# Two products of each pair swapped, and the last group's sums shared out between VectorE and GpSimd

## Chip, cores and metric

The kernel runs on one core of one Trainium2 chip. The metric is the device time of one execution in microseconds (us): 1793.84 us is the median of 3 runs of the kernel before (1793.82 to 1794.68).

In what follows PE is TensorE's matmul, DVE is VectorE, ACT is ScalarE, POOL is GpSimd, and SP is SyncE, which here only issues transfers.

## The reference

The layer count is one, so only the pooling mixer is used. All inputs are float32; the tokens are 2048 of one request and 512 of another, 1024 channels each, and the MLP is 4096 wide.

```python
def trunk(x, ...):
    h = rms_norm(x, norm_mix_g[0])
    y = pool_mixer(h, pool_w[0], pool_scale[0])   # centred means over 2, 4, 8, 16 tokens, less the token,
    x = x + y                                     # then a 256x256 product for each of 4 channel groups
    h = rms_norm(x, norm_mlp_g[0])
    a = relu(h @ w_up)                            # 1024 -> 4096
    x = x + (a * a) @ w_down                      # 4096 -> 1024
    return rms_norm(x, final_norm_g)
```

## The kernel before, in words

**Tiling.** The 2560 tokens are 5 groups of 512 (`GROUPS`; `LAST` is the fifth). The MLP's 4096 inner channels are taken 512 at a time: 8 steps per group (`PAIRS`), 40 steps in all (`STEPS`). A step n computes four up tiles (`up_tile(4n)` to `up_tile(4n+3)`, 24 matmuls each) and, beside them, the down product of step n-1. The last step's products stand alone at the end.

**Precision.** Every float32 operand is split in a high part (cast by ACT) and a low part (the difference, by DVE), and each product is three matmuls: high by high, high by low, low by high. `split_wu`, `split_w`, `split_a`, `split_h2` and `split_pooled` are such pairs, one half in ACT's program and one half of the same name in DVE's.

**Seven products.** The down product of a step is a 2x2 block product by Strassen's scheme in Winograd's form, with seven products P1 to P7 of 12 matmuls each in place of eight. Their order on PE is the tuple at line 39, `P1, P5, P6, P3, P4, P7, P2`. Left operands are quadrants of the activation `a_raw` or sums of them in one shared tile `s_sum`, which `sum_a` rewrites for P5, P6, P3 and P7 one after the other, each time when the product before has been split. Right operands are quadrants of `w_down` or sums of them (`sum_w`, tiles `t_sum` and `wd_raw`); those of the first group's 56 products are split once, stored to a cache in HBM by `store_w` and loaded again by `load_w` in later groups. SP issues both in the order of product numbers.

**Ring.** Products go to PSUM in pairs of banks, two pairs in turn (`ring_pair`). A product may start when the one two turns before it has been added by DVE to its accumulator in `m_acc` (`evict`); `ring_full` and `ring_read` count the two. `TURN` numbers the turns; in the steps that mix the next group's tokens two turns of the pooling product follow the sixth product.

**Combining.** After a group's eighth step, seven sums of 128x1024 (`combine(g, 1)` to `combine(g, 7)`, lines 844 to 866) turn the seven accumulators into four quadrants: P2 + P1 is the upper left; P3 + P5 + (P6 + P1) the upper right; with P7 + (P6 + P1) the lower left is that less P4, and the lower right is that plus P5. `evict` of the last step waits for those sums that must stand before it, since it adds to the same tile. Then, for each of four row tiles, ACT takes the mean square (`final_stats`, line 592), POOL takes the power -1/2 (`rms`, two small instructions), DVE multiplies by it and by the gain (`finish`), and SP stores. For groups 0 to 3 this lies in `boundary`, beside the next group's first step; for the last group it is the end of the kernel.

**Order.** Each engine has its own program, written out by hand: `step`, `boundary` and the lines after the loops. An engine executes in that order, and a waiting instruction holds everything behind it. In `boundary`, PE transposes the next group's normed tokens in four pairs of blocks (`transpose`), each pair ahead of one of the first four products; ACT and DVE split each block (`split_h2`, tiles h_hi and h_lo), and the first up tile waits for all eight. In the steps that mix, POOL takes the window sums (`window_sums`, line 346).

Of the kernel before, what the change touches and what calls it, by code (L numbers as in the profile page):

```python
# [6 lines left out]
P = 128  # L7
# [31 lines left out]
P1, P5, P6, P3, P4, P7, P2 = range(7)  # L39
# [23 lines left out]
FIRST_OUTS = WINDOWS * TT  # L63

# [16 lines left out]
def ring_turns():  # L81

    turns, at = {}, 0
    for n in range(STEPS + 1):
        for k in range(NP if n > 0 else 0):
            turns[NP * (n - 1) + k] = at
            at += 1
            if k == P7 and n < STEPS and pooled_window(n) is not None:
# [27 lines left out]
def build(nc, x, halos, w_up, w_down, pool_w, pool_scale, g_mix, g_mlp, g_fin, ends, bands, ident_in,  # L116
# [8 lines left out]
    with ctx:  # L125
# [66 lines left out]
        ms_f = sb("ms_f", [P, TT])  # L192
        me_f = sb("me_f", [P, TT])
# [90 lines left out]
        combined = sem("combined")  # L284
        p4_begun = sem("p4_begun")
# [70 lines left out]
        def _(sp):  # L356
# [50 lines left out]
            def store(g):  # L407
                for i, j in enumerate(end_order(g)):
# [71 lines left out]
        def _(act):  # L480
# [111 lines left out]
            def final_stats(g, r):  # L592

                squares = dt_hi[:, :, :]
                if r == 0:
                    act.wait_ge(combined, NP * g + 4)
                    act.wait_ge(ring_read, TURN[NP * (PAIRS * (g + 1) - 1) + P2] + 1)
                else:
                    act.wait_ge(combined, NP * (g + 1))
                for j in (2 * r, 2 * r + 1):  # L600
                    i = end_order(g).index(j)
                    if i > 0:
                        act.wait_ge(ms_f_done, TT * g + i)
                    nc.scalar.activation(squares, out_rows(j), ACT.Square, scale=D ** -0.5,
                                         accum_out=ms_f[:, j:j + 1]).then_inc(ms_f_done, 1)
# [100 lines left out]
            def boundary(n):  # L706
# [37 lines left out]
            for k in range(2, NP):  # L744
                split_a(NP * (STEPS - 1) + k)
            final_stats(LAST, 0)
            final_stats(LAST, 1)

        @block.vector
        def _(dve):  # L750
# [67 lines left out]
            def evict(q):  # L818
# [6 lines left out]
                if s == PAIRS - 1 and k in (P7, P2):  # L825
                    dve.wait_ge(combined, NP * g + {P2: 1, P7: 5}[k])
# [3 lines left out]
                if s > 0:  # L830
# [11 lines left out]
            def combine(g, i):  # L842
# [12 lines left out]
                elif i == 4:  # L855
                    dve.wait_ge(combined, NP * g + 3)
# [7 lines left out]
                elif i == 7:  # L864
                    dve.wait_ge(combined, NP * g + 6)
# [34 lines left out]
            def finish(g):  # L900
                dve.wait_ge(g_fin_in, 16)
                for i, j in enumerate(end_order(g)):
# [62 lines left out]
            def step(n):  # L965
# [5 lines left out]
                if n > 0:  # L971
# [42 lines left out]
            def boundary(n):  # L1014
# [16 lines left out]
                split_a(q0 + P3)  # L1031
                evict(q0 + P6)
                split_w(q0 + P4)
# [4 lines left out]
                split_w(q0 + P7)  # L1038
                evict(q0 + P3)
                split_a(q0 + P7)  # L1040
# [30 lines left out]
            combine(LAST, 1)  # L1071
# [340 lines left out]
```

## Time and profile before

| | |
|---|---|
| median of 3 runs | 1793.84 us |
| profiled execution, own time | 1795.25 us |
| profiled execution, span from first to last instruction | 1793.4 us |
| mean granted TensorE clock | 0.993 |
| PE busy | 1756.7 us (98% of the span) |
| DVE busy | 1123.0 us (63%) |
| ACT busy | 761.6 us (42%) |
| POOL busy | 158.9 us (9%) |

Busy time is the time in which at least one instruction of the engine ran; a busy PE is not PE at its peak. The times in the rows below are microseconds from the start of the span of the profiled execution. A row of a timeline has start, duration, engine, line of the source, operation, tile written <- tiles read, shape and count; in square brackets, where it is given, is the time that the engine stood idle before it and the instruction that ended the wait.

### The profile page before, as it was taken

Reading aid. Unit: us, or ns where it says so; the run is one execution under the profiler, and the core shown is the slowest. Engines: PE = TensorE matmul, PEld = TensorE weight load, DVE = VectorE, ACT = ScalarE, POOL = GpSimd, SP = SyncE. Lnnn points to the kernel's source line nnn. Section 1 sums busy time; section 2 is a strip of 40 time slices with the busy share of each in tenths; the row PEclk is TensorE's granted clock in tenths of the full one; section 3 lists DMA queues with packets and bytes.
Section 4 is the critical chain, followed back from the end, with each engine's and each line's share of the span. In section 5 each row is a group of like instructions: output and inputs, shape, how many; then the busy total and the mean of one; then the engine's idle time right before and its main releaser. Section 6 shows DMA issues by size and latency. Waiting matters only on the chain.

```text
span 1793.4 us, 20892 instructions
## 1 busy us (share of the span) xinstructions
PE 1756.7 (98%) x8118; PEld 1462.1 (82%) x8118; DVE 1123.0 (63%) x1178; ACT 761.6 (42%) x1186; POOL 158.9 (9%) x139
## 2 busy tenths in 40 slices
PE   8999999999999999999999999999999999999996
PEld 7887887778888888888888888888888888888885
DVE  5687888787555565755655647555556575545447
ACT  5546555554343334344433344443333543333232
POOL 3000112001001120010011200000112010000001
PEclk9999999999999999999999999999999999999998
DMA  7597766668866666668666665786665657666654
GB/s 256 209 343 272 265 256 251 256 241 324 298 236 221 221 223 219 244 231 297 239 221 221 222 219 200 274 301 221 222 222 210 240 201 273 245 219 240 233 201 163
DMA packets 80902, 432.67 MB, mean 241 GB/s; under 512 B 8860, under 2 KB 10780, under 8 KB 42916
## 3 DMA queue, kind: packets, MB, share of 16 engines
q1 hardware_dynamic: 57764, 347.44, 52.3%
q10 hardware_dynamic: 23040, 83.90, 13.5%
q8 instruction: 65, 1.06, 0.2%
q14 instruction: 33, 0.27, 0.0%
HBM read 360.00 MB, written 71.30 MB: 240 GB/s over the span
## 4 chain that ended last, share of the span: by engine, by line
PE 87%; DVE 7%; DMA 2%; ACT 2%; issue 1%; POOL 0%; ACTq 0%; SPq 0%; POOLq 0%; DVEq 0%
PE up_ps L1168 15%; PE up_ps L1170 15%; PE up_ps L1169 15%; PE ring_ps L1187 12%; PE ring_ps L1189 12%; PE ring_ps L1188 12%; DVE w_slot L764 1%; DVE m_acc L831 1%; PE ring_ps L1212 1%; DVE a_slot L772 1%; PE ring_ps L1214 1%; PE ring_ps L1213 1%; DVE wu_lo L755 1%; PE mix_ps L1197 1%; DMA wd_raw<-w_down 1%
## 5 line engine op out<-in xcount | busy, mean ns | idle before, releaser
L755 DVE TENSOR_TENSOR wu_lo<-wu_raw,wu_hi 128x1024 fp32r<-128x1024 f32 x158 | 195.8, 1239 | 579.0 <-ACT wu_hi L495 578.9
L1168 PE MATMUL up_ps<-h_hi,wu_hi 128*128 128x512 f32 x1280 | 501.4, 392 | 0.6 <-DVE h_lo L896 0.6
L1170 PE MATMUL up_ps<-h_hi,wu_lo 128*128 128x512 f32 x1280 | 498.4, 389 | 0.0
L1169 PE MATMUL up_ps<-h_lo,wu_hi 128*128 128x512 f32 x1280 | 498.4, 389 | 0.0
L532 ACT ACTIVATE a_raw<-up_ps 128x512 f32<-128x512 f32 x160 | 95.3, 596 | 507.0 <-PE up_ps L1170 506.9
L831 DVE TENSOR_TENSOR m_acc<-ring_ps,m_acc 128x1024 f32<-128x1024 f32 x245 | 298.7, 1219 | 18.7 <-PE ring_ps L1189 18.4
L1187 PE MATMUL ring_ps<-w_slot,a_slot 128*128 128x512 f32 x760 | 297.3, 391 | 1.1 <-DVE m_acc L831 1.1
L1189 PE MATMUL ring_ps<-w_slot,a_slot 128*128 128x512 f32 x760 | 296.6, 390 | 0.0
L1188 PE MATMUL ring_ps<-w_slot,a_slot 128*128 128x512 f32 x760 | 296.4, 390 | 0.0
L1170 PEld LDWEIGHTS up_ps<-h_hi,wu_lo 128*128 128x128 f32 x1280 | 240.3, 188 | 50.2
L1168 PEld LDWEIGHTS up_ps<-h_hi,wu_hi 128*128 128x128 f32 x1280 | 240.3, 188 | 49.3 <-DVE h_lo L896 1.2
L1169 PEld LDWEIGHTS up_ps<-h_lo,wu_hi 128*128 128x128 f32 x1280 | 240.4, 188 | 48.5
L524 ACT CAST a_slot<-s_sum 128x512 fp32r<-128x512 f32 x160 | 99.5, 622 | 280.3 <-PE ring_ps L1189 98.5
L1187 PEld LDWEIGHTS ring_ps<-w_slot,a_slot 128*128 128x128 f32 x760 | 143.1, 188 | 31.1 <-issue 1.5
L1189 PEld LDWEIGHTS ring_ps<-w_slot,a_slot 128*128 128x128 f32 x760 | 143.0, 188 | 29.8
L1188 PEld LDWEIGHTS ring_ps<-w_slot,a_slot 128*128 128x128 f32 x760 | 143.0, 188 | 29.5
L495 ACT CAST wu_hi<-wu_raw 128x1024 fp32r<-128x1024 f32 x160 | 165.5, 1034 | 0.0
L1187 PE MATMUL ring_ps<-w_more,a_slot 128*128 128x512 f32 x360 | 140.6, 391 | 0.1
L1189 PE MATMUL ring_ps<-w_more,a_slot 128*128 128x512 f32 x360 | 140.2, 389 | 0.0
L1188 PE MATMUL ring_ps<-w_more,a_slot 128*128 128x512 f32 x360 | 140.1, 389 | 0.0
L772 DVE TENSOR_TENSOR a_slot<-s_sum,a_slot 128x512 fp32r<-128x512 f32 x160 | 134.1, 838 | 3.4 <-ACT a_slot L524 3.4
L524 ACT CAST a_slot<-a_raw 128x512 fp32r<-128x512 f32 x120 | 74.6, 621 | 105.0 <-PE ring_ps L1189 104.8
(136 smaller groups left out, 1641.2 us busy)
## 6 DMA issues: line engine op xcount, KB each, us to landing
w_slot<-w_cache SPq DMA_DIRECT2D x134, 1024.0 KB, 5.1
w_more<-w_cache SPq DMA_DIRECT2D x90, 1024.0 KB, 5.1
wu_raw<-w_up ACTq DMA_DIRECT2D x160, 512.0 KB, 3.2
w_cache<-w_slot SPq DMA_DIRECT2D x56, 1024.0 KB, 4.9
wd_raw<-w_down SPq DMA_DIRECT2D x16, 1024.0 KB, 9.5
xr<-x SPq DMA_DIRECT2D x20, 512.0 KB, 7.3
out<-m_acc SPq DMA_DIRECT2D x20, 512.0 KB, 5.7
pw_slot<-pw_cache SPq DMA_DIRECT2D x16, 512.0 KB, 4.4
```

The lines of the kernel that those rows point to most:

```text
L495: nc.scalar.copy(wu_hi[:, u % FT, :, :], wu_raw[:, u % FT, :, :]).then_inc(wu_hi_done, 1)
L524: nc.scalar.copy(a_slot[:, q % A_SLOTS, 0, :, :], a_source(q)).then_inc(a_hi_done, 1)
L532: nc.scalar.activation(a, up_ps[:, u % FT, :], ACT.Relu).then_inc(relu_done, 1)
L755: nc.vector.tensor_tensor(wu_lo[:, u % FT, :, :], wu_raw[:, u % FT, :, :], wu_hi[:, u % FT, :, :].bitcast(f32), ALU.subtract).then_inc(wu_ ...
L772: nc.vector.tensor_tensor(a_slot[:, i, 1, :, :], a_source(q), a_slot[:, i, 0, :, :].bitcast(f32), ALU.subtract).then_inc(a_lo_done, 1)
L831: nc.vector.tensor_tensor(dst, src, dst, ALU.add).then_inc(ring_read, 1)
L1168: nc.tensor.matmul(o, hi, h2_hi[:, d, :], start=(d == 0), stop=False)
L1169: nc.tensor.matmul(o, hi, h2_lo[:, d, :], start=False, stop=False)
L1170: last = nc.tensor.matmul(o, lo, h2_hi[:, d, :], start=False, stop=(d == DT - 1))
L1187: nc.tensor.matmul(dst, a_hi, hi, start=(k == 0), stop=False)
L1188: nc.tensor.matmul(dst, a_hi, lo, start=False, stop=False)
L1189: last = nc.tensor.matmul(dst, a_lo, hi, start=False, stop=(k == 1))
```

## The change

**Order of the products.** The tuple becomes `P1, P5, P6, P3, P7, P4, P2`: P7 is the fifth and P4 the sixth. The programs of ACT and DVE follow in `step` and `boundary`; in `boundary` DVE issues `sum_a(n-1, P7)` ahead of the eviction of P6, ACT casts P7's operand ahead of `split_h2` of blocks 6 and 7, and combine steps 5 and 6 come ahead of the evictions of P7 and P4. In the last step of a group P4's eviction subtracts: combine step 6 is taken before it.

**The last group.** Sums 1, 3, 2 and 5 are made by POOL (`last_sums`, a counter of their own), sums 4, 6 and 7 by DVE. The row tiles are finished in the order 2, 3, 0, 1, as in the other groups. ACT takes the squares of the upper right quadrant's halves of row tiles 0 and 1 when sum 4 stands (`last_stats`), and later only the other halves; POOL adds the two.

```diff
-P1, P5, P6, P3, P4, P7, P2 = range(7)
+P1, P5, P6, P3, P7, P4, P2 = range(7)
...
+END_ORDER = (2, 3, 0, 1)
+POOL_SUMS = (1, 3, 2, 5)
+DVE_SUMS = (4, 6, 7)
...
+        def wait_combined(eng, g, i):
+            if g < LAST:
+                eng.wait_ge(combined, NP * g + i)
+            elif i in POOL_SUMS:
+                eng.wait_ge(pool_combined, POOL_SUMS.index(i) + 1)
+            else:
+                eng.wait_ge(combined, NP * g + DVE_SUMS.index(i) + 1)
...
             def final_stats(g, r):
...
+                    wait_combined(act, g, 7)
+                    act.wait_ge(ring_read, TURN[q0 + P4] + 1)
...
+                    halves = 1 if g == LAST and r == 0 else NH
+                    nc.scalar.activation(dt_hi[:, 0:halves, :], out_rows(j)[:, 0:halves, :], ACT.Square,
+                                         scale=D ** -0.5, accum_out=ms_f[:, j:j + 1]).then_inc(ms_f_done, 1)
+
+            def last_stats():
+                wait_combined(act, LAST, 4)
+                for j in range(2):
+                    if j > 0:
+                        act.wait_ge(ms_end_done, j)
+                    nc.scalar.activation(dt_lo[:, 0:1, :], out_rows(j)[:, 1:2, :], ACT.Square,
+                                         scale=D ** -0.5, accum_out=ms_end[:, j:j + 1]).then_inc(ms_end_done, 1)
...
 (ACT, boundary)
                 split_a(q0 + P3)
+                split_w(q0 + P7)
+                split_a(q0 + P7)
+                split_h2(g, 6)
+                split_h2(g, 7)
                 split_w(q0 + P4)
                 split_a(q0 + P4)
-                split_h2(g, 6)
-                split_h2(g, 7)
-                split_w(q0 + P7)
-                split_a(q0 + P7)
                 split_w(q0 + P2)
...
 (ACT, the end)
+            last_stats()
+            final_stats(LAST, 1)
             final_stats(LAST, 0)
-            final_stats(LAST, 1)
...
 (DVE, evict)
-                if s == PAIRS - 1 and k in (P7, P2):
-                    dve.wait_ge(combined, NP * g + {P2: 1, P7: 5}[k])
+                if s == PAIRS - 1 and k in (P7, P4, P2):
+                    wait_combined(dve, g, {P7: 5, P4: 6, P2: 1}[k])
+                if q == PRODUCTS - NP + P3:
+                    wait_combined(dve, g, 3)
...
+                if s == PAIRS - 1 and k == P4:
+                    nc.vector.tensor_tensor(dst, dst, src, ALU.subtract).then_inc(ring_read, 1)
+                elif s > 0:
...
 (DVE, boundary)
                 split_a(q0 + P3)
+                sum_a(n - 1, P7)
                 evict(q0 + P6)
-                split_w(q0 + P4)
+                split_w(q0 + P7)
                 split_h2(g, 6)
                 split_h2(g, 7)
-                sum_a(n - 1, P7)
+                split_a(q0 + P7)
+                split_w(q0 + P4)
+                evict(q0 + P3)
                 split_a(q0 + P4)
-                split_w(q0 + P7)
-                evict(q0 + P3)
-                split_a(q0 + P7)
                 split_w(q0 + P2)
                 for i in range(1, 5):
                     combine(g - 1, i)
                 split_wu(4 * n + 2)
-                evict(q0 + P4)
-                split_a(q0 + P2)
                 combine(g - 1, 5)
                 evict(q0 + P7)
+                split_a(q0 + P2)
+                combine(g - 1, 6)
+                evict(q0 + P4)
                 split_wu(4 * n + 3)
                 split_a(q0 + NP + P1)
-                combine(g - 1, 6)
                 combine(g - 1, 7)
...
 (DVE, the end)
             sum_a(STEPS - 1, P3)
-            combine(LAST, 1)
             evict(q0 + P5)
             split_a(q0 + P3)
             sum_a(STEPS - 1, P7)
             evict(q0 + P6)
+            split_a(q0 + P7)
+            evict(q0 + P3)
             split_a(q0 + P4)
-            combine(LAST, 2)
-            evict(q0 + P3)
-            split_a(q0 + P7)
-            combine(LAST, 3)
+            combine(LAST, 4)
+            evict(q0 + P7)
             split_a(q0 + P2)
-            combine(LAST, 4)
+            combine(LAST, 6)
             evict(q0 + P4)
-            combine(LAST, 5)
-            evict(q0 + P7)
+            combine(LAST, 7)
             evict(q0 + P2)
-            combine(LAST, 6)
-            combine(LAST, 7)
             finish(LAST)
...
 (POOL)
+            def last_sums():
+                q0 = NP * (STEPS - 1)
+                p1, p2, p3, p5, p6, p7 = (product_sum(k) for k in (P1, P2, P3, P5, P6, P7))
+                pool.wait_ge(ring_read, TURN[q0 + P1] + 1)
+                nc.gpsimd.tensor_tensor(p2, p2, p1, ALU.add).then_inc(pool_combined, 1)
+                pool.wait_ge(ring_read, TURN[q0 + P5] + 1)
+                nc.gpsimd.tensor_tensor(p3, p3, p5, ALU.add).then_inc(pool_combined, 1)
+                pool.wait_ge(ring_read, TURN[q0 + P6] + 1)
+                nc.gpsimd.tensor_tensor(p6, p6, p1, ALU.add).then_inc(pool_combined, 1)
+                wait_combined(pool, LAST, 2)
+                nc.gpsimd.tensor_tensor(p7, p7, p6, ALU.add).then_inc(pool_combined, 1)
+                pool.wait_ge(ms_end_done, 2)
+                nc.gpsimd.tensor_tensor(me_end[:, :], ms_end[:, :], eps[:, 0:2], ALU.add).then_inc(me_end_done, 1)
+                pool.wait_ge(me_end_done, 1)
```

## Rows read from the trace of the kernel before

**Rows 1.** The page's chain that ended last, share of the span by engine.

```profile
PE 87%; DVE 7%; DMA 2%; ACT 2%; issue 1%; POOL 0%; ACTq 0%; SPq 0%; POOLq 0%; DVEq 0%
```

**Rows 2.** Busy us by stretch: length, PE, PEld, DVE, ACT, POOL, clock, DMA, GB/s.

```profile
400.00:1740.00 1340.00, 1339.35 (x6137) 1113.95 (x6138) 775.27 (x809) 531.51 (x827) 105.53 (x86) 1.00 0.66 239
1740.00:1793.40 53.40, 37.76 (x164) 30.26 (x163) 33.65 (x35) 12.03 (x20) 6.68 (x8) 0.90 0.42 161
```

**Rows 3.** Timeline of the boundary at step 16: DVE, ACT and PE around block 7.

```profile
743.97 0.68 DVE L772 TENSOR_TENSOR a_slot<-s_sum,a_slot 128x512 fp32r<-128x512 f32 x1
...
745.70 1.40 DVE L896 SCALAR_TENSOR_TENSOR h_lo<-mix_ps,g_mlp_c,h_hi 128x512 fp32r<-128x512 f32 x2
747.02 0.68 DVE L816 TENSOR_TENSOR s_sum<-a_raw 128x512 f32<-128x512 f32 x1
...
744.71 1.26 ACT L589 ACTIVATE h_hi<-mix_ps,g_mlp_c 128x512 fp32r<-128x512 f32 x2
...
747.57 0.39 PE L1168 MATMUL up_ps<-h_hi,wu_hi 128*128 128x512 f32 x1
```

**Rows 4.** Timeline of the boundary at step 8: DVE and PE around block 7.

```profile
396.24 1.22 DVE L831 TENSOR_TENSOR m_acc<-ring_ps,m_acc 128x1024 f32<-128x1024 f32 x1
...
398.50 1.40 DVE L896 SCALAR_TENSOR_TENSOR h_lo<-mix_ps,g_mlp_c,h_hi 128x512 fp32r<-128x512 f32 x2
...
399.96 0.50 PE L1168 MATMUL up_ps<-h_hi,wu_hi 128*128 128x512 f32 x1 [0.57 <-DVE h_lo L896]
```

**Rows 5.** Timeline of a step with POOL's window sums: POOL and DVE.

```profile
1007.36 1.94 POOL L346 TENSOR_TENSOR sums<-ht 128x1052 f32<-128x1052 f32 x1 [37.06 <-ACT ht L568]
1007.53 2.32 DVE L772 TENSOR_TENSOR a_slot<-s_sum,a_slot 128x512 fp32r<-128x512 f32 x1
1009.39 2.26 POOL L346 TENSOR_TENSOR sums<-sums 128x1048 f32<-128x1048 f32 x1
1009.89 2.31 DVE L816 TENSOR_TENSOR s_sum<-a_raw 128x512 f32<-128x512 f32 x1
...
1013.94 1.23 DVE L755 TENSOR_TENSOR wu_lo<-wu_raw,wu_hi 128x1024 fp32r<-128x1024 f32 x1 [1.74 <-ACT wu_hi L495]
1014.06 3.36 POOL L346 TENSOR_TENSOR sums<-sums 128x1024 f32<-128x1024 f32 x1
1015.08 1.22 DVE L831 TENSOR_TENSOR m_acc<-ring_ps,m_acc 128x1024 f32<-128x1024 f32 x1
```

**Rows 6.** POOL's window sums by tile: count, duration ns min/median/max.

```profile
L346 POOL TENSOR_TENSOR sums<-sums x24: 2223/2246/3358, 210.8 to 1361.5; 128x1024 f32<-128x1024 f32 x12, 128x1032 f32<-128x1032 f32 x4, 128x1048 f32<-128x1048 f32 x4, 128x1040 f32<-128x1040 f32 x4
```

**Rows 7.** Timeline of the last step's products: DVE, then PE's late starts.

```profile
1760.88 1.23 DVE L831 TENSOR_TENSOR m_acc<-ring_ps,m_acc 128x1024 f32<-128x1024 f32 x1 [0.17 <-PE ring_ps L1189]
...
1762.74 0.69 DVE L814 TENSOR_TENSOR s_sum<-a_raw,s_sum 128x512 f32<-128x512 f32 x1
1763.35 1.22 DVE L848 TENSOR_TENSOR m_acc<-m_acc 128x1024 f32<-128x1024 f32 x1
...
1779.07 1.23 DVE L831 TENSOR_TENSOR m_acc<-ring_ps,m_acc 128x1024 f32<-128x1024 f32 x1 [0.84 <-PE ring_ps L1189]
...
1766.35 0.50 PE L1187 MATMUL ring_ps<-w_more,a_slot 128*128 128x512 f32 x1
...
1775.98 0.47 PE L1187 MATMUL ring_ps<-w_slot,a_slot 128*128 128x512 f32 x1 [1.14 <-DVE m_acc L831]
```

**Rows 8.** Timeline of the end: ACT's first square, POOL's power, DVE's multiplies.

```profile
1780.39 1.06 ACT L604 ACTIVATE dt_hi<-m_acc 128x1024 fp32r<-128x1024 f32 x1 [7.55 <-DVE m_acc L831]
...
1783.47 1.28 DVE L904 SCALAR_TENSOR_TENSOR m_acc<-m_acc,rs_f,g_fin_b 128x1024 f32<-128x1024 f32 x1 [0.78 <-POOL rs_f L1095]
1783.60 1.56 POOL L1095 TENSOR_TENSOR rs_f<-me_f,power 128x1 f32<-128x1 f32 x1
...
1785.20 1.28 DVE L904 SCALAR_TENSOR_TENSOR m_acc<-m_acc,rs_f,g_fin_b 128x1024 f32<-128x1024 f32 x1 [0.44 <-POOL rs_f L1095]
...
1788.65 1.28 DVE L904 SCALAR_TENSOR_TENSOR m_acc<-m_acc,rs_f,g_fin_b 128x1024 f32<-128x1024 f32 x1 [0.44 <-POOL rs_f L1095]
```

More of the change, by code:

```diff
@@ L87, in ring_turns @@
             at += 1
-            if k == P7 and n < STEPS and pooled_window(n) is not None:
+            if k == P4 and n < STEPS and pooled_window(n) is not None:
                 for half in range(2):
@@ L192, in build @@
         ms_f = sb("ms_f", [P, TT])
+        ms_end = sb("ms_end", [P, 2])
+        me_end = sb("me_end", [P, 2])
         me_f = sb("me_f", [P, TT])
@@ L284, in build @@
         combined = sem("combined")
+        pool_combined = sem("pool_combined")
+        ms_end_done = sem("ms_end_done")
+        me_end_done = sem("me_end_done")
         p4_begun = sem("p4_begun")
@@ L407, in store @@
             def store(g):
-                for i, j in enumerate(end_order(g)):
+                for i, j in enumerate(END_ORDER):
                     sp.wait_ge(final_done, TT * g + i + 1)
@@ L592, in final_stats @@
             def final_stats(g, r):
[L594 removed]
+                q0 = NP * (PAIRS * (g + 1) - 1)
                 if r == 0:
[L596 to L599 removed]
+                    wait_combined(act, g, 4)
+                    act.wait_ge(ring_read, TURN[q0 + P2] + 1)
+                else:
+                    wait_combined(act, g, 7)
+                    act.wait_ge(ring_read, TURN[q0 + P4] + 1)
                 for j in (2 * r, 2 * r + 1):
[L601 removed]
+                    i = END_ORDER.index(j)
                     if i > 0:
                         act.wait_ge(ms_f_done, TT * g + i)
[L604 to L605 removed]
+                    halves = 1 if g == LAST and r == 0 else NH
[8 more added lines that the diff above has]
+                                         scale=D ** -0.5, accum_out=ms_end[:, j:j + 1]).then_inc(ms_end_done, 1)
             act.wait_ge(const_set, 3)
@@ L901, in finish @@
                 dve.wait_ge(g_fin_in, 16)
-                for i, j in enumerate(end_order(g)):
+                for i, j in enumerate(END_ORDER):
                     dve.wait_ge(rs_f_done, TT * g + i + 1)
@@ L1044, in boundary @@
                 split_wu(4 * n + 2)
-                evict(q0 + P4)
-                split_a(q0 + P2)
                 combine(g - 1, 5)
                 evict(q0 + P7)
+                split_a(q0 + P2)
+                combine(g - 1, 6)
+                evict(q0 + P4)
                 split_wu(4 * n + 3)
                 split_a(q0 + NP + P1)
-                combine(g - 1, 6)
                 combine(g - 1, 7)
@@ L1075, in _ @@
             evict(q0 + P6)
+            split_a(q0 + P7)
+            evict(q0 + P3)
             split_a(q0 + P4)
-            combine(LAST, 2)
-            evict(q0 + P3)
-            split_a(q0 + P7)
-            combine(LAST, 3)
+            combine(LAST, 4)
+            evict(q0 + P7)
             split_a(q0 + P2)
-            combine(LAST, 4)
+            combine(LAST, 6)
             evict(q0 + P4)
-            combine(LAST, 5)
-            evict(q0 + P7)
+            combine(LAST, 7)
             evict(q0 + P2)
-            combine(LAST, 6)
-            combine(LAST, 7)
             finish(LAST)
@@ L1105, in final_rms @@
             def final_rms(g):
-                for i, j in enumerate(end_order(g)):
+                for i, j in enumerate(END_ORDER):
                     c = slice(j, j + 1)
                     pool.wait_ge(ms_f_done, TT * g + i + 1)
-                    rms(ms_f[:, c], me_f[:, c], rs_f[:, c], 1, me_f_done, TT * g + i + 1, rs_f_done)
+                    halves = g == LAST and j < 2
+                    rms(ms_f[:, c], me_f[:, c], rs_f[:, c], 1, me_f_done, TT * g + i + 1, rs_f_done,
+                        me_end[:, c] if halves else None)
+            def last_sums():
[12 more added lines that the diff above has]
+                pool.wait_ge(me_end_done, 1)
             def next_sums(m, w):
```

14 lines of the change are left out of this document (7 added, 7 removed).

## The prediction, made before the kernel was run

> **What bounds the kernel now.** I read the chain of waits first, by engine: TensorE (PE) holds 87% of it [rows 1]. Then the busy time by stretch: from 400 to 1740 us PE is busy 1339.35 of 1340 us, so nothing but PE bounds the middle; in the last 53.4 us it is busy 37.76 [rows 2]. So an edit can pay in two places only: where PE stands still (the end, and the first group), or where it now barely does not. The second place is the group boundary. At n=16 the first up-projection matmul starts at 747.57; the last h2_lo block that it waits for is ready at 745.70 + 1.40 = 747.10, so PE has 0.47 us to spare [rows 3]. Boundaries 24 and 32 show the same pattern. At n=8 there is nothing to spare: PE already waited 0.57 us there and started at 399.96, 0.06 us behind h2_lo [rows 4]. The end is a chain of VectorE (DVE), PE, ScalarE (ACT), GpSimd (POOL) and the last store [rows 7, 8].
>
> **The swap of P4 and P7 in ordinary steps: nothing.** Seven products per step, the same instructions and the same ring; the fifth and sixth change places. P7's left operand comes from s_sum, so its cast now needs `sum_a(P7)` one turn earlier. In the worst step, with POOL's window sums beside it, `sum_a(P7)` ends at 1009.89 + 2.31 = 1012.20 [rows 5]; ACT casts the fifth operand only behind the next up tile's relu, square and weight cast, so I count 0. Weight casts get easier (P7's source is ready before P4's). On SP's queue the store and load order goes by product number, and `load_raw` stands behind `store_w(q0+5)`, which already waits for the sixth product's weights, so no transfer moves. Bounds: -0.1 and +0.1 per step that has POOL sums, 16 steps, -1.6 to +1.6; I take 0.
>
> **The boundaries: +2.1 us.** DVE now issues `sum_a(P7)` ahead of `evict(P6)` and `split_h2(6..7)`, not behind. ACT now casts P7's operand ahead of `split_h2(6..7)`, and that cast waits for this very sum.
> At n=16: `split_a(P3)` ends at 743.97 + 0.68 = 744.65; the sum (0.68, now waiting for that split) ends at 745.37; ACT casts until about 746.0 and starts `split_h2(6)` near 745.95, where it started at 744.71 before [rows 3]. Its two blocks take 1.26, so the second is ready at 747.2; DVE's part behind it (half of 1.40, plus handover) ends at 748.0, PE starts at 748.05, not 747.57: +0.48. By DVE's queue alone it would be 0.68 more work less 0.47 of slack, +0.2 to +0.3: the lower bound. Three boundaries: 3 x 0.48 = 1.44.
> At n=8 `evict(P6)` starts at 396.24 and the blocks at 398.50 [rows 4]. The sum ahead of it, with its wait, shifts all of it by 0.7, and there is no slack: +0.7.
> PE has no idle time behind a boundary that could take this up [rows 2], so the two add: 2.14 us. Bounds 1.3 (DVE's queue alone) and 2.8 (0.7 everywhere). The combine steps 5 and 6 move ahead of evictions, 2 x 1.14 us, but PE's seventh product comes a whole up tile later (24 matmuls), so they are hidden; without this cover a boundary would pay up to 2.3.
>
> **The end, without contention: -3.8 us.** Of seven sums of 128x1024 (1.22 each, the first at 1763.35 [rows 7]) four leave DVE, a further one goes ahead of P4's last eviction, and behind the last eviction (P2, at 1779.07) no sum is left where two stood. PE's waits before P3 and P2 (1.14 us of them in the row at 1775.98, 0.2 at 1766.35) would be gone with handovers, so P2's eviction could start at about 1777.3 in place of 1779.07; `combine(7)`, then ahead of it, ends at that time too. ACT's squares would start at 1777.3, not behind that eviction at 1780.39 [rows 8]: 3.1 us earlier. Two of them are half as wide (about 0.5 less each, from 1.06), of which some 0.7 reaches the last multiply: it would start at 1784.8, not 1788.65. That is the lower bound.
>
> **What POOL's sums cost DVE.** A POOL sum of 1024 takes 2.25 us (median of 24 [rows 6]); the nearest other form took 1.94. Beside it every DVE instruction with both inputs in SBUF stands: the split of 128x512 that started at 1007.53 took 2.32 us rather than 0.68, and `s_sum` at 1009.89 took 2.31; each ended about 0.55 us behind the POOL sum (1007.36 + 1.94; 1009.39 + 2.26). Evictions, with one input in PSUM, do not: 1.22 at 1015.08 beside a sum [rows 5]. In the end, what stands on PE's path is just such splits and `s_sum` instructions. In order:
> - `evict(P1)` ends at 1762.1 [rows 7]; POOL adds P2 from 1762.2 to 1764.45. `sum_a(P3)`, issued at 1762.74 as before, now ends at 1765.0 rather than 1763.4. Then eviction of P5, `split_a(P3)` at 1766.1 to 1766.75; PE starts P3 at 1766.8, not 1766.35.
> - POOL's P3 sum (released by that eviction at 1766.15) holds `sum_a(P7)` until 1769.05; `evict(P6)`, then `split_a(P7)` until 1770.8. PE starts its fifth product at 1770.85, 1.3 us after the fourth has ended.
> - POOL's P6 sum (1770.3 to 1772.55) holds `split_a(P4)` until 1773.1, still ahead of PE (1773.55); POOL's P7 sum then holds `combine(4)` until 1774.9, so it ends at 1776.0.
> - `evict(P7)` needs both: 1776.0 to 1777.2. `split_a(P2)` until 1777.8; PE starts P2 at 1777.85, not 1775.98. Then `combine(6)`, `evict(P4)`, `combine(7)` until 1781.3, last eviction 1781.2 to 1782.4.
> - ACT squares rows 2 and 3 from 1781.4 (before: first square 1780.39), rows 0 and 1 half wide until 1785.35. The first multiply starts at 1783.5 (before 1783.47), the second at 1785.5 (before 1785.20), since POOL's little sum now stands behind the first multiply; the third and fourth follow at the old spacing of 1.73, because `rs_f` takes 1.56 beside a multiply [rows 8]. The last starts at 1789.0, not 1788.65: **+0.3 us**.
> So the squares taken early and the two sums fewer behind P2 just pay for a PE that ends 1.9 us later.
>
> Whether a POOL sum is itself held is the open price. The one issued at 1009.39, while DVE's delayed split ran until 1009.85, still took 2.26; the one at 1014.06, behind a 1024-wide DVE instruction (1013.94 to 1015.17), took 3.36 [rows 5]. I take the first, since each of the four here meets a 512-wide DVE split. The Trainium skill, "SBUF — State Buffer", "Who interferes with whom", has it that a DVE instruction with two SBUF inputs and a GpSimd instruction that reads SBUF exclude each other for the whole instruction, whoever is second blocking fully. For DVE the trace agrees (2.32 and 2.31); for the sum at 1009.39 it does not (2.26, where full blocking for 0.46 us would have given about 2.7). By the rule the four sums would start up to 4 x 0.46 = 1.8 us later in total, and the end with them: +2.1 in place of +0.3.
>
> **Sum.** 2.14 + 0.3 = +2.4 us: the profiled execution, span 1793.4 and own time 1795.25, would become 1795.8 and 1797.7. The median of the runs is 1793.84, 1.4 below the profiled time; on it, **1796.3 us**, +0.13%. A measurement here tells less than 0.2% (3.6 us) from nothing, so the forecast is "no difference that can be told".
>
> **Rivals.**
> (1) POOL's sums hide fully: the four take 9 us in a stretch of 17, and DVE has less to do. The boundaries stay: 2.1 - 3.8 = -1.7, 1792.1. For it: evictions pass freely, and DVE is relieved of 4 x 1.14 us. Against it: the two rows of 2.3 us, on the same kinds of instruction.
> (2) Slower: POOL's sums are held in turn. Place: the four sums between 1762 and 1777. Price: 0.46 each behind a split, up to 1.1 where a 1024-wide DVE instruction gets in first, as at 1014.06 (3.36 against 2.25). It decides from the moment when a sum is issued behind a DVE instruction rather than ahead of it; three of my four are. 1.8 to 3.4 us on top: 1798.1 to 1799.7, +0.24 to +0.33%.
> (3) The boundaries cost nothing, because ACT or DVE has slack that the rows hide: +0.3, 1794.1. Against it: 0.47 us at n=16 and none at n=8.
> (4) Both 1 and 3: -3.8, 1790.0, faster by 0.21%; this is the change doing all that it can.
>
> **Chances.** Forecast 0.48 (its own range 1794.8 to 1797.9: a POOL sum of 1.94 gives -1.0, boundaries of 1.3 another -0.8; boundaries of 2.8 and handovers +1.6). Rival 1: 0.17; 2: 0.18; 3: 0.10; 4: 0.07. The range 1791.5 to 1799.0 leaves out rival 4, the fast edge of rival 1 and the upper half of rival 2, some 0.18. Faster by over 0.2% (below 1790.3): rival 4 and the edge of 1, 0.10. Slower by over 0.2% (above 1797.4): rival 2 and the top of the forecast, 0.25. Within: 0.65.
>
> **What would show it.** Boundaries: the first up matmul waits for h2_lo at all four, some 0.5 us at the last three and 1.3 at the first; the last step's first eviction then starts about 2.1 us later. End: `s_sum` and split instructions of over 2 us beside four POOL sums; PE idle about 1.2 us before its fifth product and 1.5 before P2. The prediction is wrong if the boundaries show no new wait, if those DVE instructions stay at 0.7 us (rival 1), or if POOL's sums take 3 us and more (rival 2).

## The result, and the profile after

The changed kernel takes 1800.5 us (median of 9 runs, 1798.4 to 1802.34). Against the kernel before, timed beside it, that is a ratio of 1.0033, 95% interval 1.0024 to 1.0042: about 5.9 us slower, which can be told from no change. One of the nine runs of the kernel before took 2526.03 us and does not count in the ratio. The forecast was 1796.3 with a range up to 1799.0, so the time lies outside it. The profiled execution took 1800.93 us, its span is 1799.1 (before: 1795.25 and 1793.4), and the mean granted TensorE clock is 0.993 in both.

The page of the kernel after, span and busy time by engine:

```profile
span 1799.1 us, 20913 instructions
...
PE 1758.3 (98%) x8118; PEld 1461.9 (81%) x8118; DVE 1126.6 (63%) x1174; ACT 762.4 (42%) x1190; POOL 169.0 (9%) x144
```

Busy time by stretch, the kernel after (columns as in [rows 2]):

```profile
400.00:1740.00 1340.00, 1337.13 (x6122) 1111.00 (x6123) 773.48 (x807) 531.20 (x827) 105.49 (x86) 1.00 0.66 238
1740.00:1799.10 59.10, 41.62 (x180) 33.01 (x178) 39.50 (x34) 13.71 (x26) 16.98 (x13) 0.92 0.42 160
```

In the middle PE now stands still for 2.87 us where it stood 0.65 [rows 2]. In the last stretch POOL has 16.98 us of work and DVE 39.50. Four sums went from DVE to POOL, and yet DVE is busier over the whole span: 1126.6 us, before 1123.0. An instruction that is held counts as busy while it stands, so this points at holds; the rows of the end below show them.

PE's waits over the whole kernel (engine, tile, line, and what it waited for: us in total, times, longest), the two that are new or grown:

```profile
PE ring_ps L1231 <- DVE a_slot L796: 4.6, 3, 2.1
...
PE up_ps L1212 <- DVE h_lo L926: 2.3, 4, 1.3
```

**Where the 5.7 us of span are.** ACT's relu of each of the 160 up tiles makes a clock for the comparison: subtract its start in one trace from its start in the other.

| stretch | before | after | difference |
|---|---|---|---|
| start-up, relus' shift in step 7 | | | +0.57 |
| boundary at step 8, growth of the shift | | | +0.62 |
| boundary at step 16 | | | +0.67 |
| boundary at step 24 | | | +0.65 |
| boundary at step 32 | | | +0.67 |
| steps between the boundaries, together | | | +0.30 |
| last step's first `s_sum` to the last multiply | 31.85 | 34.08 | +2.23 |
| sum | | | +5.71 |

Between the boundaries the shift grows by 0.02, 0.16, 0.12 and 0.00 us in the four groups, the larger two in the steps with window sums; what makes it grow there was not followed, but in experiment 1, which keeps the swap, it moves by 0.04 at most in each, so the swap alone does not cost it. The start-up is taken as scatter, not the change: in step 0, ahead of the first product, the shift is already +0.95, and in the profiles of the experiments below it lies there anywhere from -1.1 to +1.4. This leaves 2.61 us for the boundaries (forecast 2.14), 0.30 for the ordinary steps (forecast 0) and 2.23 for the end (forecast 0.3).

**A boundary.** Timeline of the kernel after at step 16, DVE, ACT and PE around block 7, as in [rows 3]:

```profile
745.17 0.68 DVE L796 TENSOR_TENSOR a_slot<-s_sum,a_slot 128x512 fp32r<-128x512 f32 x1
745.89 0.69 DVE L840 TENSOR_TENSOR s_sum<-a_raw 128x512 f32<-128x512 f32 x1
746.50 1.22 DVE L859 TENSOR_TENSOR m_acc<-ring_ps,m_acc 128x1024 f32<-128x1024 f32 x1
747.86 1.41 DVE L926 SCALAR_TENSOR_TENSOR h_lo<-mix_ps,g_mlp_c,h_hi 128x512 fp32r<-128x512 f32 x2
...
746.61 0.62 ACT L536 CAST a_slot<-s_sum 128x512 fp32r<-128x512 f32 x1 [2.68 <-DVE s_sum L840]
747.14 1.26 ACT L601 ACTIVATE h_hi<-mix_ps,g_mlp_c 128x512 fp32r<-128x512 f32 x2
...
749.32 0.50 PE L1212 MATMUL up_ps<-h_hi,wu_hi 128*128 128x512 f32 x1 [0.35 <-DVE h_lo L926]
```

The line to read is ACT's cast: it stands 2.68 us for `s_sum` and starts h_hi only at 747.14. From there the path runs through DVE's h_lo to the first up matmul, which waits 0.35 us where it did not wait before [rows 3]. The rows look the same at steps 24 and 32. At step 8 the wait is 1.26 (0.57 before [rows 4]):

```profile
401.15 0.50 PE L1212 MATMUL up_ps<-h_hi,wu_hi 128*128 128x512 f32 x1 [1.26 <-DVE h_lo L926]
```

**The end.** POOL's and DVE's timelines of the kernel after, the last step (to set against [rows 5 to 7]):

```profile
1765.66 2.77 POOL L1143 TENSOR_TENSOR m_acc<-m_acc 128x1024 f32<-128x1024 f32 x1 [287.61 <-DVE m_acc L859]
1770.20 2.77 POOL L1145 TENSOR_TENSOR m_acc<-m_acc 128x1024 f32<-128x1024 f32 x1 [1.76 <-DVE m_acc L859]
1774.73 2.77 POOL L1147 TENSOR_TENSOR m_acc<-m_acc 128x1024 f32<-128x1024 f32 x1 [1.76 <-DVE m_acc L859]
1777.58 2.74 POOL L1149 TENSOR_TENSOR m_acc<-m_acc 128x1024 f32<-128x1024 f32 x1
```

```profile
1760.28 0.69 DVE L832 TENSOR_TENSOR s_sum<-a_raw 128x512 f32<-128x512 f32 x1 [4.98 <-ACT a_raw L546]
...
1765.50 0.68 DVE L796 TENSOR_TENSOR a_slot<-s_sum,a_slot 128x512 fp32r<-128x512 f32 x1
1766.22 2.77 DVE L838 TENSOR_TENSOR s_sum<-a_raw,s_sum 128x512 f32<-128x512 f32 x1
...
1770.04 0.68 DVE L796 TENSOR_TENSOR a_slot<-s_sum,a_slot 128x512 fp32r<-128x512 f32 x1
1770.75 2.76 DVE L840 TENSOR_TENSOR s_sum<-a_raw 128x512 f32<-128x512 f32 x1
...
1774.57 0.68 DVE L796 TENSOR_TENSOR a_slot<-s_sum,a_slot 128x512 fp32r<-128x512 f32 x1
1775.17 1.21 DVE L859 TENSOR_TENSOR m_acc<-ring_ps,m_acc 128x1024 f32<-128x1024 f32 x1
1776.31 1.75 DVE L796 TENSOR_TENSOR a_slot<-a_raw,a_slot 128x512 fp32r<-128x512 f32 x1
1777.98 3.43 DVE L887 TENSOR_TENSOR m_acc<-m_acc 128x1024 f32<-128x1024 f32 x1
...
1786.58 1.22 DVE L859 TENSOR_TENSOR m_acc<-ring_ps,m_acc 128x1024 f32<-128x1024 f32 x1
...
1794.36 1.28 DVE L934 SCALAR_TENSOR_TENSOR m_acc<-m_acc,rs_f,g_fin_b 128x1024 f32<-128x1024 f32 x1 [0.44 <-POOL rs_f L1121]
```

Read the two fences side by side. POOL's first sum is issued at 1765.66, 0.16 us into a split that runs until 1765.50 + 0.68 = 1766.18. The sum takes 2.77: the 0.52 us to the end of the split, and 2.25, the figure of [rows 6]. It then holds DVE's `s_sum`, which takes 2.77 rather than 0.69 and ends 0.56 us behind it. The second and third sums are issued just as far into a split (1770.20 against 1770.04, 1774.73 against 1774.57), and the fourth 0.48 us ahead of the end of one (1777.58 against 1776.31 + 1.75): 2.74 - 0.48 = 2.26. A whole eviction, with one input in PSUM, ran beside the third sum (1775.17) and none beside the first two, and all three took 2.77. The third sum holds a split (1.75 in place of 0.68), the fourth holds sum 4 (3.43 in place of 1.22). So each engine holds the other in turn, four times. The products pay on PE (timeline, the kernel after, its three late starts):

```profile
1770.78 0.50 PE L1231 MATMUL ring_ps<-w_more,a_slot 128*128 128x512 f32 x1 [1.01 <-DVE a_slot L796]
...
1775.31 0.50 PE L1231 MATMUL ring_ps<-w_more,a_slot 128*128 128x512 f32 x1 [1.52 <-DVE a_slot L796]
...
1783.19 0.50 PE L1231 MATMUL ring_ps<-w_slot,a_slot 128*128 128x512 f32 x1 [2.05 <-DVE a_slot L796]
```

What the change does gain is there too. From P2's eviction to the last multiply the kernel before took 1788.65 - 1779.07 = 9.58 us [rows 7, 8]; now it is 1794.36 - 1786.58 = 7.78, as forecast (7.8). But the stretch up to that eviction grew from 22.27 to 26.30: +4.03 - 1.80 = +2.23.

### The profile page after: what moved, and what is told of

It is laid out like the page before. It is cut to its first block, busy times and chain, and to the rows that moved or that the text cites. A ratio compares the mean times of both kernels' runs of the same rounds, so it can differ in the third digit from the quotient of the medians.

```text
span 1799.1 us, 20913 instructions
## 1 busy us (share of the span) xinstructions
PE 1758.3 (98%) x8118; PEld 1461.9 (81%) x8118; DVE 1126.6 (63%) x1174; ACT 762.4 (42%) x1190; POOL 169.0 (9%) x144
## 4 chain that ended last, share of the span: by engine, by line
PE 87%; DVE 7%; ACT 2%; issue 1%; DMA 1%; POOL 0%; ACTq 0%; SPq 0%; POOLq 0%; DVEq 0%
PE up_ps L1212 16%; PE up_ps L1214 15%; PE up_ps L1213 15%; PE ring_ps L1233 12%; PE ring_ps L1232 12%; PE ring_ps L1231 12%; DVE m_acc L859 1%; PE ring_ps L1256 1%; DVE h_lo L926 1%; DVE a_slot L796 1%; PE ring_ps L1258 1%; PE ring_ps L1257 1%; DVE w_slot L788 1%; PE mix_ps L1241 1%; DMA w_cache<-w_slot 1%
## 5 line engine op out<-in xcount | busy, mean ns | idle before, releaser
L859 DVE TENSOR_TENSOR m_acc<-ring_ps,m_acc 128x1024 f32<-128x1024 f32 x240 | 292.4, 1219 | 17.9 <-PE ring_ps L1233 17.5
L1231 PEld LDWEIGHTS ring_ps<-w_slot,a_slot 128*128 128x128 f32 x760 | 143.0, 188 | 32.2 <-DVE a_slot L796 2.9
```

What stands on the lines that cost most here:

```text
L859: nc.vector.tensor_tensor(dst, src, dst, ALU.add).then_inc(ring_read, 1)
L1231: nc.tensor.matmul(dst, a_hi, hi, start=(k == 0), stop=False)
```

## Experiments

The theory: the boundaries' time comes from the new order of `sum_a(P7)` and of its cast alone; the end's from POOL's sums and DVE's two-input instructions holding each other. The rivals: that the swap costs elsewhere, that the boundary is paid on one engine's queue alone, and that a POOL sum is simply slow in this place and not held.

**1. The boundaries' order put back on ACT and DVE (`e1_bound`).**

```diff
 (ACT, boundary)
-                split_a(q0 + P7)
                 split_h2(g, 6)
                 split_h2(g, 7)
+                split_a(q0 + P7)
 (DVE, boundary)
-                sum_a(n - 1, P7)
                 evict(q0 + P6)
                 split_w(q0 + P7)
                 split_h2(g, 6)
                 split_h2(g, 7)
+                sum_a(n - 1, P7)
                 split_a(q0 + P7)
```

> The changed kernel with the boundaries' old order: in DVE's program the P7 sum stands behind the split of blocks 6 and 7 again, in ACT's the cast of P7's operand too; P7 stays ahead of P4. Theory (the boundaries lost 2.9 us because that sum and that cast stand ahead of the last two blocks): no wait of the first up matmul for h2_lo at steps 16, 24, 32, about 0.6 left at step 8; the last step's first eviction 2.8 us earlier than in the changed kernel, span 1799.1 - 2.9 = 1796.2, 2.3 to 3.5 over the kernel before. Rival (the exchange of P4 and P7 in the ordinary steps costs it, or the combine steps that moved ahead of evictions): the loss stays, span 1798.5 to 1799.1.

Measured: 1798.05 us, ratio 1.0018 (1.0009 to 1.0027); the span is 1795.6, 2.2 over the kernel before where 2.3 to 3.5 was expected. Against the kernel before, the relus' shift grows by 0.10 us from step 7 to the last step, where it grew by 2.91 (2.61 at the boundaries, 0.30 between them) in the kernel after: the loss is gone. The first up matmul after the boundaries at 8 and 16 (timeline of this kernel) waits as it did before, and not at all:

```profile
399.82 0.50 PE L1212 MATMUL up_ps<-h_hi,wu_hi 128*128 128x512 f32 x1 [0.55 <-DVE h_lo L926]
...
747.49 0.39 PE L1212 MATMUL up_ps<-h_hi,wu_hi 128*128 128x512 f32 x1
```

The end is unchanged (34.21 us, after 34.08). So the boundaries' cost is this order and nothing else of the swap.

**2. Only ACT's boundary order put back (`e1a_act`).** ACT casts P7's operand behind `split_h2(6..7)` again; DVE keeps the new order.

```diff
 (ACT, boundary)
-                split_a(q0 + P7)
                 split_h2(g, 6)
                 split_h2(g, 7)
+                split_a(q0 + P7)
```

> Only ACT's order at the boundaries is the old one (blocks 6 and 7 ahead of the cast of P7's operand); DVE still makes the P7 sum ahead of P6's eviction. If the path over ACT is the one that ends last: at steps 16, 24 and 32 the start of the up tile comes 0.2 to 0.3 us earlier than in the changed kernel, and 0.4 to 0.5 of the 0.7 stays as DVE's own queue; step 8 unchanged; in all -0.6 to -0.9 us. If DVE's queue alone decides: 0.

Measured, one execution: 1800.94 us, the shifts at the four boundaries 0.67, 0.48, 0.44 and 0.46 (after: 0.62, 0.67, 0.65, 0.67). The last three are each some 0.2 us cheaper, the first is not. So at 16, 24 and 32 ACT's cast is what ends last, but with it gone DVE's queue, which has the same 0.7 us more ahead of h_lo, is only 0.2 behind it. The two paths lie close together; to have the time back, both orders must go back. The total, one run, does not show 0.6 us; only the relus do.

**3. POOL's first three sums released later (`e3_gate`).** The sums stay on POOL, but each is issued when a two-input DVE instruction has just ended, not just after one has begun.

```diff
                 pool.wait_ge(ring_read, TURN[q0 + P1] + 1)
+                pool.wait_ge(s_done, 4 * (STEPS - 1) + 3)
                 nc.gpsimd.tensor_tensor(p2, p2, p1, ALU.add).then_inc(pool_combined, 1)
                 pool.wait_ge(ring_read, TURN[q0 + P5] + 1)
+                pool.wait_ge(s_done, 4 * (STEPS - 1) + 4)
                 nc.gpsimd.tensor_tensor(p3, p3, p5, ALU.add).then_inc(pool_combined, 1)
                 pool.wait_ge(ring_read, TURN[q0 + P6] + 1)
+                pool.wait_ge(a_lo_done, q0 + P7 + 1)
                 nc.gpsimd.tensor_tensor(p6, p6, p1, ALU.add).then_inc(pool_combined, 1)
```

> The changed kernel with POOL's first three sums released later: the first behind the s_sum of P3, the second behind the s_sum of P7, the third behind the split of P7's operand, so that each starts beside an eviction and not behind a split. Theory (POOL's sum takes 2.25 and was held 0.5 by the split that ran when it was issued): the first three take 2.25, the two s_sum instructions 0.7 rather than 2.77, P3 starts on PE without a wait, and the end comes 1.5 to 2 us earlier: span 1797.1 to 1797.6. Rival (a sum in place in m_acc takes 2.77 of its own): they stay at 2.77, and the end comes 0 to 0.8 earlier.

Measured: 1799.66 us, ratio 1.0027 (1.0016 to 1.0037); the end takes 32.92 us, 1.16 less than after. Timelines of this kernel, POOL and then DVE:

```profile
1766.87 2.40 POOL L1144 TENSOR_TENSOR m_acc<-m_acc 128x1024 f32<-128x1024 f32 x1 [289.00 <-DVE s_sum L838]
1770.69 2.40 POOL L1147 TENSOR_TENSOR m_acc<-m_acc 128x1024 f32<-128x1024 f32 x1 [1.42 <-DVE s_sum L840]
1773.78 2.40 POOL L1150 TENSOR_TENSOR m_acc<-m_acc 128x1024 f32<-128x1024 f32 x1 [0.70 <-DVE a_slot L796]
1776.26 2.72 POOL L1152 TENSOR_TENSOR m_acc<-m_acc 128x1024 f32<-128x1024 f32 x1
...
1766.03 0.69 DVE L838 TENSOR_TENSOR s_sum<-a_raw,s_sum 128x512 f32<-128x512 f32 x1
1766.89 1.23 DVE L859 TENSOR_TENSOR m_acc<-ring_ps,m_acc 128x1024 f32<-128x1024 f32 x1 [0.17 <-PE ring_ps L1236]
1768.04 1.78 DVE L796 TENSOR_TENSOR a_slot<-s_sum,a_slot 128x512 fp32r<-128x512 f32 x1
...
1774.69 2.04 DVE L796 TENSOR_TENSOR a_slot<-a_raw,a_slot 128x512 fp32r<-128x512 f32 x1
```

The three sums that were moved take 2.40, not 2.77; each begins with no two-input DVE instruction running. The fourth, still issued beside a split (1774.69 + 2.04 = 1776.73), takes 2.72. So the sums were held, and the moment of issue decides. `s_sum` is back at 0.69, but the hold went to the next instruction: the split waits for POOL's end in its place, 1.78 us, and PE still waits 0.30, 0.81 and 2.05 us before the three products that were late after the change (1.01, 1.52, 2.05). A sum that is not held takes 2.40, 0.15 more than the 2.25 that a held one takes once it is let go, so the gain is 3 x 0.37 = 1.1, not the 1.5 to 2 that was expected. The eviction beside these sums is not what costs the 0.15: the third sum of the kernel after had one beside it too, and took 0.52 + 2.25 like the others.

**4. All seven sums on DVE (`e2_dve`).** The order of products, the boundaries and the early squares stay.

```diff
-POOL_SUMS = (1, 3, 2, 5)
-DVE_SUMS = (4, 6, 7)
+POOL_SUMS = ()
+DVE_SUMS = (1, 2, 3, 5, 4, 6, 7)
...
 (DVE, the end)
             sum_a(STEPS - 1, P3)
+            combine(LAST, 1)
             evict(q0 + P5)
...
             split_a(q0 + P7)
+            combine(LAST, 2)
             evict(q0 + P3)
             split_a(q0 + P4)
+            combine(LAST, 3)
+            combine(LAST, 5)
             evict(q0 + P7)
             split_a(q0 + P2)
             combine(LAST, 4)
             combine(LAST, 6)
             evict(q0 + P4)
             combine(LAST, 7)
             evict(q0 + P2)
...
```

> The changed kernel with all seven sums of the last group on DVE (order 1, 2, 3, 5, 4, 6, 7), POOL has none; product order, subtracting eviction and early squares stay. Theory (beside DVE instructions with two SBUF inputs a POOL sum saves DVE nothing, it only moves the time into waits): no DVE instruction of the last step over 1.3 us, PE starts P2 within 1.2 us of the end of P4, and the last multiply starts some 3 us earlier than in the changed kernel: span 1795.5 to 1796.5. Rival (DVE is the bound and the four sums were 4.6 us of relief): the end comes later than in the changed kernel by 1 us or more, span 1800 and over.

Measured: 1797.44 us, ratio 1.0015 (1.0006 to 1.0024); the end takes 31.31 us, 2.77 less than after and 0.54 less than before. The shifts at the boundaries stay, at 0.70 to 0.72. Four sums more on DVE are 4 x 1.14 = 4.56 us of its time, and yet the end is shorter: after the change the holds cost DVE 2.08 and 2.07 us on two `s_sum`, 1.07 on a split and 2.21 on sum 4, 7.4 in all. PE's one late start is P2's (timeline of this kernel):

```profile
1777.62 0.50 PE L1225 MATMUL ring_ps<-w_slot,a_slot 128*128 128x512 f32 x1 [1.00 <-DVE a_slot L796]
```

**5. Both undone (`f1_both`):** the edits of 1 and 4 in one kernel; the order of products and the early squares are what is left of the change.

```diff
 (ACT, boundary)
-                split_a(q0 + P7)
                 split_h2(g, 6)
                 split_h2(g, 7)
+                split_a(q0 + P7)
 (DVE, boundary)
-                sum_a(n - 1, P7)
                 evict(q0 + P6)
...
+                sum_a(n - 1, P7)
...
-POOL_SUMS = (1, 3, 2, 5)
-DVE_SUMS = (4, 6, 7)
+POOL_SUMS = ()
+DVE_SUMS = (1, 2, 3, 5, 4, 6, 7)
...
```

> Both repairs together: boundaries in the old order and all seven sums of the last group on DVE; P7 ahead of P4, the subtracting eviction and the early squares stay. If the two causes are all of it and add up: no drift against the kernel before between 410 and 1740 us, the stretch from the last step's first s_sum to the last multiply 31.3 us (31.85 before, 34.08 in the changed kernel), time -0.5 us against the kernel before, ratio 0.9990 to 1.0005. Rival (a part of the loss lies elsewhere, in what both repairs keep): 2 us or more over the kernel before, ratio 1.001 and over.

Measured: 1795.37 us beside 1794.74 for the kernel before, ratio 1.0001 (0.9992 to 1.0009). Its end takes 31.30, 0.55 less than before, and from 410 to 1740 us its relus keep their shift within 0.11. So the two causes add up, and there is no third that the rows or the time (within 1.6 us) would show. The 0.5 us under the kernel before that was expected can't be told in the time.

**6. The sums where DVE has time (`f2_late`).** As 5, with sums 1, 2, 5, 6, 7 and 3 in this order, and sum 4 behind the first multiply; ACT squares rows 2 and 3 first, then the left halves of rows 0 and 1, then the right ones.

```diff
 (DVE, the end, against experiment 5)
...
             split_a(q0 + P4)
-            combine(LAST, 3)
             combine(LAST, 5)
             evict(q0 + P7)
             split_a(q0 + P2)
-            combine(LAST, 4)
             combine(LAST, 6)
             evict(q0 + P4)
             combine(LAST, 7)
+            combine(LAST, 3)
             evict(q0 + P2)
-            finish(LAST)
+            finish(LAST, range(0, 1))
+            combine(LAST, 4)
+            finish(LAST, range(1, 4))
 (ACT, the end)
-            last_stats()
             final_stats(LAST, 1)
+            last_stats()
             final_stats(LAST, 0)
...
```

> As the kernel with both repairs, but on DVE the sums are taken in the order in which something waits for them: 1, 2, 5, 6, 7 ahead of 3 and 4, and sum 4 stands between the first and second multiply; ACT squares rows 2 and 3 first, then the left halves of rows 0 and 1, then the right halves. Theory (DVE's queue is the bound of the end, so the order of its sums decides): PE starts P2 without a wait of more than 0.3 us, and the last multiply starts 29.3 to 30.3 us behind the last step's first s_sum: 1.5 to 2.5 us under the kernel before. Rival (the chain of POOL's powers and DVE's multiplies at 1.73 each bounds the end): 31 us and over, no gain against the kernel with both repairs.

Measured: 1793.9 us beside 1794.74, ratio 0.9995 (0.9986 to 1.0004). The end takes 30.17 us, 1.68 less than before, as expected. DVE's timeline of this kernel from P2's eviction on:

```profile
1778.55 1.22 DVE L859 TENSOR_TENSOR m_acc<-ring_ps,m_acc 128x1024 f32<-128x1024 f32 x1
1779.68 1.28 DVE L934 SCALAR_TENSOR_TENSOR m_acc<-m_acc,rs_f,g_fin_b 128x1024 f32<-128x1024 f32 x1
1780.88 1.22 DVE L887 TENSOR_TENSOR m_acc<-m_acc 128x1024 f32<-128x1024 f32 x1
1782.60 1.28 DVE L934 SCALAR_TENSOR_TENSOR m_acc<-m_acc,rs_f,g_fin_b 128x1024 f32<-128x1024 f32 x1 [0.51 <-POOL rs_f L1126]
...
1786.32 1.28 DVE L934 SCALAR_TENSOR_TENSOR m_acc<-m_acc,rs_f,g_fin_b 128x1024 f32<-128x1024 f32 x1 [0.44 <-POOL rs_f L1126]
```

The first multiply stands right behind the eviction, because its row's squares were taken before; the fourth sum fills DVE's wait for POOL's power. It is the best version found, and by its trace the end is shorter, but its time can't be told from that of the kernel before.

**7. One sum alone on POOL, issued at the best moment (`f3_one`).** As 5, with sum 1 on POOL behind `s_sum` of P3.

```diff
-POOL_SUMS = ()
-DVE_SUMS = (1, 2, 3, 5, 4, 6, 7)
+POOL_SUMS = (1,)
+DVE_SUMS = (2, 3, 5, 4, 6, 7)
...
             sum_a(STEPS - 1, P3)
-            combine(LAST, 1)
 (POOL)
+                pool.wait_ge(ring_read, TURN[q0 + P1] + 1)
+                pool.wait_ge(s_done, 4 * (STEPS - 1) + 3)
+                nc.gpsimd.tensor_tensor(p2, p2, p1, ALU.add).then_inc(pool_combined, 1)
```

> As the kernel with both repairs, with one sum only (P2 + P1) on POOL, released behind the s_sum of P3 so that it starts beside an eviction and is not held itself. Theory (a POOL sum of 2.4 us can lie beside one eviction of 1.14 only; the rest of it DVE's next split stands still, which is what DVE saves): the split of P3's operand takes 1.6 to 1.8 us rather than 0.68, and the last multiply moves by less than 0.4 us either way. Rival (DVE's load is the bound and a sum off it is a gain): the end comes 0.8 to 1.2 us earlier than with both repairs.

Measured: 1794.23 us beside 1794.74, ratio 0.9995 (0.9986 to 1.0004); the end takes 31.53, 0.23 more than in 5. POOL's sum and the DVE instructions beside it (timeline of this kernel):

```profile
1764.29 2.40 POOL L1145 TENSOR_TENSOR m_acc<-m_acc 128x1024 f32<-128x1024 f32 x1 [289.00 <-DVE s_sum L838]
...
1764.31 1.23 DVE L857 TENSOR_TENSOR m_acc<-ring_ps,m_acc 128x1024 f32<-128x1024 f32 x1 [0.17 <-PE ring_ps L1229]
1765.45 1.78 DVE L796 TENSOR_TENSOR a_slot<-s_sum,a_slot 128x512 fp32r<-128x512 f32 x1
```

The sum off DVE saves it 1.14 us; the split behind the eviction takes 1.10 longer. An eviction covers 1.14 of the sum's 2.40, and the rest is paid back.

## Why the prediction was wrong

**The step that failed** is the one the prediction put as "Whether a POOL sum is itself held is the open price". It took the sum at 1009.39 as one that was not held, because its 2.26 us equal the 2.25 that it used for a free sum. But 2.25 is no free sum's time: all 24 instructions behind that median [rows 6] were issued while a two-input DVE instruction was running. Four of them, with 1.00 to 1.10 us of it left, took 3.27 to 3.36: a hold and about 2.26. The other 20, with 0.47 left, took 2.22 to 2.26: a hold and 1.75 to 1.80. The twenty are a quicker kind of add, whose two inputs lie 2 or 4 elements apart in one tile (`window_sums`); the nearest kind that was not held, 1 element apart, took 1.89 to 1.94, as at 1007.36 [rows 5]. In the four they lie 8 apart, and after the hold these run as long as the last group's sums, whose inputs are two accumulators. On this reading, which is taken from rows and was not tried, the sum at 1009.39 was held for 0.47 us like the rest, and that its total comes out at the figure of the slower kind is a coincidence. In both kinds the time behind a hold is some 0.15 less than the time of an add that was not held (1.75 to 1.80 against 1.89 to 1.94, 2.25 against 2.40). Why inputs close together are added faster, and where the 0.15 lies, no run shows.

One of the twenty, with the unheld add ahead of it and the split that ran at its issue (timelines of the kernel before, POOL, then DVE):

```profile
1264.90 1.91 POOL L346 TENSOR_TENSOR sums<-ht 128x1028 f32<-128x1028 f32 x1 [42.46 <-ACT ht L568]
1266.88 2.22 POOL L346 TENSOR_TENSOR sums<-sums 128x1024 f32<-128x1024 f32 x1
...
1265.07 2.28 DVE L772 TENSOR_TENSOR a_slot<-s_sum,a_slot 128x512 fp32r<-128x512 f32 x1
```

The split ends at 1265.07 + 2.28 = 1267.35, 0.47 us into the sum of 2.22.

The other row, at 1014.06, is of the kind that counts here: it was issued 1.11 us ahead of the end of a DVE instruction (1013.94 + 1.23), and 1.11 + 2.25 is its 3.36. I put that down to the width of the DVE instruction, not to the time that it had left. The Trainium skill, "SBUF — State Buffer", "Who interferes with whom", says that issue order decides which of the two is blocked. The four sums of the end agree with it (0.52, 0.52, 0.52 and 0.48 us held), and so does the sum at 1009.39, which the prediction counted against full blocking. With four holds of 0.46 the prediction had +2.1 for the end, and +2.23 was measured.

With that one term put right the working of the end holds. Times from the last step's first `s_sum` (1756.80 in the profile before, 1760.28 after):

| event | forecast | measured | late by |
|---|---|---|---|
| POOL's first sum ends | 7.65 | 8.15 | 0.5 |
| `sum_a(P3)` ends | 8.2 | 8.71 | 0.5 |
| `sum_a(P7)` ends | 12.25 | 13.23 | 1.0 |
| `split_a(P4)` ends | 16.3 | 17.78 | 1.5 |
| `combine(4)` ends | 19.2 | 21.13 | 1.9 |
| PE starts P2 | 21.05 | 22.91 | 1.9 |
| last multiply starts | 32.2 | 34.08 | 1.9 |

Half a microsecond is added by each sum in turn, and nothing behind the fourth. This is rival 2, at its place and, for the end, within its price (1.8 to 3.4 us on top of the forecast; 1.9 measured); it was given 0.18. It had three of the four sums behind a DVE instruction; all four were.

**Boundaries.** Mechanism right, term a little small: 2.61, not 2.14, inside the bounds of 1.3 to 2.8. At step 8 0.62 (forecast 0.7). At step 16 the matmul starts 0.54 later than the shift ahead of it explains (forecast 0.48) and, having waited, takes 0.50 us rather than 0.39; the relus show 0.67 in all. Steps 24 and 32 are like it (0.65 and 0.67), as the prediction took them to be. That a matmul behind a wait takes 0.11 longer was in no term.

**Ordinary steps, hidden combines, the tail.** Ordinary steps: 0.30 where 0 was forecast, well inside the bounds of -1.6 to +1.6. Hidden combines and tail: right, with no further wait at the boundaries and 7.78 us from P2's eviction to the last multiply.

**The sum.** 2.23 - 0.3 = 1.9 for the end, 2.61 - 2.14 = 0.5 for the boundaries and 0.3 for the ordinary steps make 2.7 us over the forecast of +2.4; the start-up's 0.57 makes the profile's +5.7. On the forecast of 1796.3 the 2.7 alone make 1799.0, the end of the range. The rest is the base: 1800.5 divided by the ratio is 1794.6, 0.8 us above the median on which the forecast was set, and some 0.7 that no term names, within the ratio's interval of 1.6 us either way. Rivals 1 and 4, in which POOL's sums hide, fall by the rows of the end and by experiment 7; rival 3 falls by the waits at the boundaries and by experiment 1. (The low end of the forecast's own range is 1794.5 by its own terms, 1796.3 - 1.0 - 0.8, not 1794.8; nothing hangs on it here.)

## What to carry to other kernels

Before moving work to GpSimd, list the VectorE instructions that will be beside it and count only the time of those that do not exclude it: here 1.14 us of eviction against 2.4 us of sum, so nothing was to be had, even at the best moment of issue. Before a row is taken as the time of a free instruction, look at what ran on the other engine when it was issued: a median of 24 rows was no guard here, since all 24 had been held. Price a contended instruction from both sides, its own hold (what the other has left when it is issued) as well as the hold that it puts on the other, and follow it along the chain, since holds on one path add up. Where an instruction is moved ahead of others, price every engine's queue that it passes through: ACT's and DVE's paths at a boundary were 0.2 us apart here, and undoing one of them gave back only that.

## What the runs showed of the hardware

**The same wait, two clocks.** PE waited 2.05 us before the last product after the change, and 2.07 in experiment 1, behind the same work. After the change PE kept its clock; in experiment 1 it lost it. Busy time over 6 us around that product, the kernel after and then experiment 1 (columns as in [rows 2]):

```profile
1781.60:1787.60 6.00, 3.02 (x12) 2.18 (x12) 5.97 (x6) 2.18 (x5) 0.20 (x1) 1.00 0.00 0
```

```profile
1778.00:1784.00 6.00, 4.44 (x12) 3.30 (x12) 5.00 (x5) 2.19 (x5) 0.20 (x1) 0.72 0.00 0
```

Twelve matmuls in both, but a mean granted clock of 0.72 in place of 1.00. At the lower level (1.2 GHz) they came 0.43 us apart, at the upper (2.4 GHz) 0.23. DVE stood idle for 1.25 us ahead of P2's eviction, and yet the end grew by 0.13 only (34.21 against 34.08): after the change DVE stands idle for 1.11 behind that eviction, until the first row's power is there, and in experiment 1 it multiplies at once. DVE's timeline of experiment 1:

```profile
1784.28 1.22 DVE L859 TENSOR_TENSOR m_acc<-ring_ps,m_acc 128x1024 f32<-128x1024 f32 x1 [1.25 <-PE ring_ps L1233]
1785.42 1.27 DVE L934 SCALAR_TENSOR_TENSOR m_acc<-m_acc,rs_f,g_fin_b 128x1024 f32<-128x1024 f32 x1
```

Two more profiles have the same wait: in experiment 2 it was 2.05 us and the clock fell (0.72 over the same 6 us), in experiment 3 it was 2.05 us and the clock stayed (1.00). So it is not the length of this wait that decides between the two clocks, and what does these runs do not show.

**A hold moves on rather than goes.** With POOL's first sum issued 1.4 us later in the last step in experiment 3, `s_sum` was back at 0.69 us, and the split behind the eviction took 1.78 in place of 0.68.
